# A decoder layer on one core: routing of the second tile's units moved between the first tile's, a 16-bit comparison, gate sums in rows, ring buffers given up one by one

## What is computed

```python
q = (hf @ w_q).reshape(T, 8, 2, 128)
sc = einsum('thpc,pkc->thpk', q, sub_keys)            # two lists of 128 key scores
v1, i1 = top_k(sc, 16)
cand = v1[:, :, 0, :, None] + v1[:, :, 1, None, :]    # pair sums
cidx = i1[:, :, 0, :, None] * 128 + i1[:, :, 1, None, :]
top, pos = top_k(cand, 16)
experts = take_along_axis(cidx, pos)                  # 128 experts for each token
gates = softmax(top)
a = gelu(einsum('cd,ced->ce', x, u[experts]))
y = einsum('ce,ced->cd', gates * a, v[experts])
```

## Time and profile before

| | |
|---|---|
| median of 3 runs | 947.8 us (945.09 to 950.91) |
| the profiled execution | 950.39 us |
| its span, first to last instruction | 948.6 us, 15685 instructions |
| mean granted TensorE clock | 0.945 |
| HBM read over the span | 343.80 MB, 364 GB/s |

### The profile page before, as it was taken

One profiled execution on the slowest core, in us unless ns is written; L12 is line 12 of the kernel. 1 busy time (PEld: TensorE's weight loads), 2 busy tenths in 40 slices (PEclk: granted clock), 3 DMA queues, 4 the chain that ended last, 5 costly groups with the idle time before them and its releaser, 6 DMA issues.

```text
span 948.6 us, 15685 instructions
## 1 busy us (share of the span) xinstructions
PE 849.3 (90%) x5808; PEld 548.5 (58%) x5808; DVE 648.5 (68%) x1485; ACT 417.2 (44%) x1049; POOL 386.9 (41%) x307
## 2 busy tenths in 40 slices
PE   8999999999988869887869999877897997998997
PEld 7999998799976524443446656342442551333333
DVE  5433686565557976887765787999989875444555
ACT  5534665544565653553433444444452332222252
POOL 1000065040004475565544435365664775343452
PEclk9999999999999999999989999787877997999999
DMA  8897533257336899999999999999899999999994
GB/s 307 229 202 210 183 125 134 89 223 266 134 111 224 350 414 404 404 415 407 342 383 414 414 412 406 373 374 366 310 397 390 376 415 415 417 414 401 402 346 187
DMA packets 55028, 303.20 MB, mean 320 GB/s; under 512 B 11515, under 2 KB 14959, under 8 KB 21777
## 3 DMA queue, kind: packets, MB, share of 16 engines
q0 software_dynamic: 37152, 225.29, 59.9%
q1 hardware_dynamic: 14968, 74.03, 21.8%
q10 hardware_dynamic: 2832, 2.88, 2.2%
HBM read 343.80 MB, written 1.54 MB: 364 GB/s over the span
## 4 chain that ended last, share of the span: by engine, by line
PE 38%; DMA 30%; DVE 15%; ACT 8%; issue 5%; POOL 3%; POOLq 0%; SPq 0%; DVEq 0%; ACTq 0%
DMA arena<-in_experts,arena 19%; PE y L1178 9%; DMA raw<-in_panels 6%; DVE late_ring L2179 5%; PE y L1249 4%; PE ps L792 4%; PE ps L794 3%; PE ps L793 3%; DVE w_lo L1748 3%; ACT w_hi L1331 2%; DMA late_ring<-in_experts,arena 2%; PE ps L835 2%; POOL arena L2387 2%; PE y L1137 1%; PE y L1302 1%
## 5 line engine op out<-in xcount | busy, mean ns | idle before, releaser
L2387 POOL DMA_INDIRECT arena<-in_experts,arena x167 | 223.5, 1338 | 168.1 <-PE ps L1181 124.9
L2179 DVE CUSTOM_DVE_ANT_0 late_ring<-arena 128x1024 f32<-128x1024 f32 x178 | 217.1, 1222 | 104.3 <-DMA arena<-in_experts,arena 100.4
L1181 PE MATMUL ps<-arena,diag 64*64 64x512 f32 x824 | 226.9, 678 | 0.0
L1178 PE MATMUL y<-arena,diag 64*64 64x512 f32 x528 | 146.2, 678 | 34.3 <-ACT diag L1565 34.2
L1178 PE MATMUL y<-late_ring,diag 64*64 64x512 f32 x424 | 118.3, 683 | 40.0 <-ACT diag L1565 39.9
L1551 ACT ACTIVATE acts<-dots 128x2 f32<-128x2 f32 x124 | 25.2, 203 | 290.5 <-DVE dots L2179 290.3
L1748 DVE TENSOR_TENSOR w_lo<-raw,w_hi 128x2048 fp32r<-128x2048 f32 x36 | 84.9, 2360 | 75.5 <-ACT w_hi L1331 75.5
L2179 DVE CUSTOM_DVE_ANT_0 late_ring<-late_ring,arena 128x1024 f32<-128x1024 f32 x73 | 89.3, 1223 | 37.2 <-DMA late_ring<-in_experts,arena 29.4
L2387 POOL DMA_INDIRECT late_ring<-in_experts,arena x55 | 71.5, 1299 | 99.9 <-PE ps L1181 89.0
L1178 PEld LDWEIGHTS y<-arena,diag 64*64 64x64 f32 x528 | 34.4, 144 | 114.3 <-ACT diag L1565 60.5
L1331 ACT CAST w_hi<-raw 128x2048 fp32r<-128x2048 f32 x37 | 70.5, 1905 | 62.7 <-DMA raw<-in_panels 49.4
(11 more groups left out here) (345 smaller groups left out, 1730.1 us busy)
## 6 DMA issues: line engine op xcount, KB each, us to landing
raw<-in_panels SPq DMA_DIRECT2D x40, 1024.0 KB, 5.1
arena<-in_panels SPq DMA_DIRECT2D x6, 1024.0 KB, 7.0
late_ring<-in_up SPq DMA_DIRECT2D x12, 512.0 KB, 8.3
late_ring<-in_experts SPq DMA_DIRECT2D x12, 512.0 KB, 7.8
x<-in_up SPq DMA_DIRECT2D x8, 512.0 KB, 8.6
x<-in_experts SPq DMA_DIRECT2D x8, 512.0 KB, 7.7
arena<-in_experts,arena POOLq DMA_INDIRECT x167, 14.4
arena<-line_scratch ACTq DMA_DIRECT2D x8, 320.0 KB, 9.0
```

What stands on the lines that cost most here:

```text
L1178: straight = pe.matmul(y[rows, t, cols], diag[rows, a % DIAGS, rows], slot(a)[rows, down], start=False, stop=False, skip_group_check=True)
L1181: across = pe.matmul(ps[to, half, :], diag[rows, b % DIAGS, rows], slot(b)[rows, down], start=first, stop=False, skip_group_check=True)
L2179: i = nc.vector.tensor_tensor_reduce(row if n < len(FIRST_BUFFERS) else products[s % GROUP], row, h_rows[:, u // PEER_HEADS, :], 1.0, 0.0, ...
L2387: nc.gpsimd.indirect_dma_start(out=slot(n), out_offset=None, in_=experts, in_offset=bass.IndirectOffsetOnAxis(ap=expert_rows(u)[:, s:s + 1 ...
```

## The change

It does these things:

- The order of routing becomes 0, 1, 2, 8, 3, 4, 9, 5, 10, 6, 7, 11, ... 15 (`ROUTED_AS`). Units 1 and 2 are early, over slots 0 to 8 and 9 to 18; all others are late, from slot 20 on, one per 8 slots (9 and 11 once each), and their steps are packed into 10 slots. Unit 15 begins at slot 120. Counts and waits go by the place in that order.
- Lists are turned and taken at slots 98 and 136; chunks begin at 110, 116, 122, 128 and then every 4 slots from 132 to 176; the down products are spread over groups 94 to 118.
- Buffers are given up one by one: 15 from slot 67, 14 from 71, 10 from 87, 11 from 97, 12 from 101. The ring has 13 or 14 buffers from slot 62 to 72, 12 or 13 to 101, and 10 from 105 on.
- There are 4 table places; the first two tables are loaded as soon as `x` is free, the next two when buffer 15 is.
- The places and 0 to 49 are compared as 16-bit values, with a 16-bit result (`is_pick`); a copy of `iota` is made once.
- Gate sums lie by block and token: PE writes its 20 columns 16 values apart, ACT copies, DVE weighs contiguous rows; the three products of `listed_gates` are one instruction.

The diff, cut:

```diff
-EARLY_ROUTED = 6
-LATE_ROUTES = {7: 78, 8: 86, 9: 94, 10: 102, 11: 110, 12: 118, 13: 127, 14: 136, 15: 145}
-LATE_STEPS = {1: 0, 2: 1, 3: 2, 4: 3, 6: 6, 7: 7, 8: 7, 9: 8, 10: 8, 12: 11, 13: 12, 14: 13}
+LATE_ROUTES = {8: 20, 3: 29, 4: 40, 9: 48, 5: 56, 10: 64, 6: 72, 7: 80, 11: 88, 12: 96, 13: 104, 14: 112, 15: 120}
+EARLY_ROUTES = {1: (0, 8), 2: (9, 18)}
+EARLY_ROUTED = len(EARLY_ROUTES)
+ROUTED_AS = {unit: n for n, unit in enumerate([0] + list(EARLY_ROUTES) + list(LATE_ROUTES))}
+LATE_STEPS = {1: 0, 2: 0, 3: 1, 4: 1, 6: 4, 7: 4, 8: 5, 9: 5, 10: 5, 12: 8, 13: 8, 14: 9}
...
-GATES_AT = {13: 1, 25: 2, 43: 3, 56: 4, 70: 5, 82: 6}
-SOFTMAX_BEHIND = {3: 2, 8: 3, 18: 4, 24: 5, 31: 6, 38: 7}
+GATES_AT = {10: 1, 19: 2}
+SOFTMAX_BEHIND = {3: 1, 8: 2}
...
-    RANKS_BEHIND[(begun + 3) // GROUP] = unit
-    TOP_BEHIND[(begun + 8) // GROUP] = unit
-    ROWS_BEHIND[(begun + 13) // GROUP] = unit
-    GATES_AT[begun + 14] = unit
+    RANKS_BEHIND[(begun + 1) // GROUP] = unit
+    TOP_BEHIND[(begun + 5) // GROUP] = unit
+    ROWS_BEHIND[(begun + 9) // GROUP] = unit
+    GATES_AT[begun + 10] = unit
...
-LISTS_BEHIND = {48: 0, 80: 1}
-LISTS_AT = {100: 0, 163: 1}
+LISTS_BEHIND = {47: 0, 66: 1}
+LISTS_AT = {98: 0, 136: 1}
...
-    begun = 114 + 6 * q if q < TOKEN_CHUNKS // 2 else 165 + 7 * (q - TOKEN_CHUNKS // 2) // 2
+    begun = 110 + 6 * q if q < 4 else 132 + 4 * (q - 4)
...
-    DOWN_BEHIND.setdefault(100 + b * 20 // BLOCKS, []).append(b)
+    DOWN_BEHIND.setdefault(94 + b * 26 // BLOCKS, []).append(b)
...
-GIVEN_BACK, GIVEN_FROM = (10, 11, 12, 14, 15), 62
+GIVEN_FROM = {15: 67, 14: 71, 10: 87, 11: 97, 12: 101}
...
-        if n == GIVEN_FROM:
-            waiting = [b for b in waiting if b not in GIVEN_BACK]
+        waiting = [b for b in waiting if GIVEN_FROM.get(b, SLOTS) > n]
         b = JOINS[n] if n in JOINS else waiting.pop(0)
-        if n < GIVEN_FROM or b not in GIVEN_BACK:
-            waiting.append(b)
+        waiting.append(b)
...
-        gate_sums = sb("gate_sums", [P, SUMS, 2, CHUNK * BLOCKS])
+        gate_sums = sb("gate_sums", [P, SUMS, BLOCKS, LISTED])
...
+        is_pick = work[:, TOPK * PAIRS // 2:].bitcast(BF16).rearrange("p (k c) -> p k c", k=TOPK)
...
-                   for at in (7 * D, 8 * D)]
-        tables = [x[:, 0, :], x[:, 1, :]] + [given[:, at:at + D] for at in (5 * D, 6 * D, 9 * D)]
+                   for at in (8 * D, 9 * D)]
+        tables = [x[:, 0, :], x[:, 1, :]] + [given[:, at:at + D] for at in (6 * D, 7 * D)]
...
-            sp.wait_ge(slot_free, LAST_GIVEN + 1)
             sp.wait_ge(ffn_sq_ready, 2 * TILES)
-            sp.wait_ge(taken["act"], taken_count(f"key_score{PEER_HEADS - 1}"))
-            sp.dma_start(count_row[:], count_in.to_broadcast([P, PEER_KEYS])).then_inc(count_in_place, 16)
             for j in range(2 * BLOCKS):
...
+                if j == TILES:
+                    sp.wait_ge(slot_free, LAST_IN[15] + 1)
+                if j == len(tables):
+                    sp.wait_ge(taken["act"], taken_count(f"key_score{PEER_HEADS - 1}"))
+                    sp.dma_start(count_row[:], count_in.to_broadcast([P, PEER_KEYS])).then_inc(count_in_place, 16)
...
+                sums = b[:, 0:CHUNK * BLOCKS].rearrange("p (b t) -> p b t", b=BLOCKS)
                 for j in range(CHUNK):
                     for piece in range(PIECES):
-                        mm = pe.matmul(b[:, j * BLOCKS:(j + 1) * BLOCKS], onehots[q % 2][:, :, j],
+                        mm = pe.matmul(sums[:, :, j], onehots[q % 2][:, :, j],
...
+                if j % 4 == 0:
+                    act.wait_ge(slot_free, LAST_IN[(14, 10, 12)[j // 4]] + 1)
...
-                late = u > EARLY_ROUTED
+                late = ROUTED_AS[u] > EARLY_ROUTED
...
-                    nc.vector.tensor_tensor(pick[:], top_atf[:].unsqueeze(2).to_broadcast([P, TOPK, PAIRS]),
-                                            iota[:].unsqueeze(1).to_broadcast([P, TOPK, PAIRS]), ALU.is_equal
+                    nc.vector.tensor_tensor(is_pick[:], top_places[:].unsqueeze(2).to_broadcast([P, TOPK, PAIRS]),
+                                            places[:].unsqueeze(1).to_broadcast([P, TOPK, PAIRS]), ALU.is_equal
...
+                elif q == 0:
+                    dve.wait_ge(slot_free, LAST_IN[11] + 1)
...
-                for piece in range(PIECES):
-                    nc.vector.tensor_tensor((gates_even, gates_odd)[k % 2][:, piece], in_block,
-                                            gate_piece[:, piece, tokens].unsqueeze(1).to_broadcast(shape), ALU.mult)
+                shape = [P, PIECES, BLOCKS, LISTED]
+                nc.vector.tensor_tensor((gates_even, gates_odd)[k % 2][:], in_block.unsqueeze(1).to_broadcast(shape),
+                                        gate_piece[:, :, tokens].unsqueeze(2).to_broadcast(shape), ALU.mult)
...
-                part_of_acts = in_block_acts[:, :, k * LISTED:(k + 1) * LISTED].rearrange(
-                    "p b (h t) -> p b h t", h=2)
-                sums = gate_sums[:, k % SUMS].rearrange("p h (t b) -> p b h t", b=BLOCKS)
-                nc.vector.tensor_tensor(part_of_acts, part_of_acts, sums, ALU.mult).then_inc(blocks_gated, 1)
+                part_of_acts = in_block_acts[:, :, k * LISTED:(k + 1) * LISTED]
+                nc.vector.tensor_tensor(part_of_acts, part_of_acts, gate_sums[:, k % SUMS], ALU.mult
```

73 lines of the change are left out of this document (42 added, 31 removed).

## The result

The median is 941.1 us (937.64 to 946.3, 20 runs) against 945.84 (942.39 to 952.16, 20 runs) for the kernel before: a ratio of 0.994, 95% interval 0.9923 to 0.9957. That is 5 us where 20 were forecast. It lies inside the range, near its upper end, and within the 1% that was called no change. The profiled execution has a span of 943.7 us, 4.9 less than before.

The account below looks back on a forecast made before the run. From about 330 to 930 us transfers bound the kernel at 415 GB/s, elsewhere DVE or PE. Terms 11 + 6 + 4.5 + 0.5 - 1 - 1 = 20 us took the median from 947.8 to 928 us; range 914 to 943.

Parts of the forecast that it names:

- What a stretch loses: Stretches below 415 GB/s: each loses its length times (415 - rate) / 415, put down to the engine that is full.
- The 11 us of the chunk stage: 598 to 700 us: DVE is the bound and 13.8 us are lost; with 2 to 3 left, 11 us gained.
- The 6 us of ring and tables: 450 to 490 us: more ring buffers and earlier tables replace 6.0 us of idle transfers; gain 6 us, 3 to 7.
- as balanced as before: no gain, no loss: Slots 74 to 114, up products: PE and transfers stay in balance, so neither gain nor loss there.
- The 4.5 us of the end: 890 to 930 us: PE bound by down products; spread over 26 groups, PE is no longer the bound, gain 4.5 us.
- The tail: From the last dot to its products: 4.1 us where some 2 are needed; 0.5 us counted, up to 2 possible.
- The start and tile 0's load: Start: units 1 and 2 press more steps between slots, 1 us lost; tile 0: DVE at 97%, 1 us lost, 0 to 6.
- rival A: Slots 20 to 74: DVE becomes the bound in tile 0, 8 us lost, 936 us, or 942; chance 0.12.
- Comparison and strided writes: DVE's 16-bit comparison stays at 0.99 us (0.57 by the one-hot's rate); PE's 48 strided gate products stay at 3.2 us.
- rival C: Chunks of gate products: strided PE writes overlap half as well, 6.8 us a chunk, 953 us, slower; chance 0.08.
- B: Chunk and down stages: the gain turns into other waits as faster DVE meets PE; 938 us, or 944; chance 0.14.
- D: 450 to 490 us: transfers were slow for another reason, the ring's part does nothing; 934 us, inside the forecast's 0.66.

Follow-up runs that it names:

- e8: Kernel after with calendar, giving-up of buffers and gate sums all as before; only early tables and 16-bit comparison stay: ratio 1.0015.
- e5: Kernel after with calendar and giving-up of buffers as before; cheaper gate sums, early tables and comparison stay: ratio 0.9945.
- e13: Kernel after with calendar and gate sums as before; ring, tables and comparison stay new: ratio 0.9991.
- e2: Kernel after with the calendar of before (routes, lists, chunks, down products at their old slots): ratio 0.9951.
- x6: Kernel after with one-hots of 8 keys in place of 128 from the third chunk on and one of three gate pieces multiplied: ratio 0.9911.
- e9: Kernel after with all tables waiting, as before, for the buffer and the last key score: ratio 0.9936.
- x4: Kernel after with half of the places compared, other picks becoming the first expert, so 13.3 MB more gathered: ratio 1.0233, 970.9 us.
- x3: Kernel after with only the first four up and four down tables loaded and reused, 18.9 MB left out: ratio 0.9705, 918.86 us.
- e7: Kernel after with up products two groups earlier, behind groups 35 to 54 in place of 37 to 56: ratio 0.992, 940.82 us.
- x1: Kernel after with one of three gate pieces multiplied, 16 gate products a chunk in place of 48: ratio 0.9932.
- e1: Kernel after with its five ring buffers given up at once at slot 62, as before: ratio 0.9945.
- e15: Kernel after with buffer 1 joining the ring at slot 192 in place of 79, nine buffers in place of ten: ratio 0.9959.

## Why the prediction was wrong

The direction was right, the size 4 times too large. The smaller mechanisms came as forecast; the terms of the three large gains did not. By its own steps:

**What a stretch loses.** This is the step that failed. I took the lost time as length x (415 - rate) / 415 and put all of it down to the one engine that was full, so that it would be had back when that engine was relieved. The three stretches gave 11 + 6 + 4.5 = 21.5 us in this way. In the chunk stage, relieving the full engine brought a part; ahead of the up products, what was won was held by the PE-bound stage behind it; over the down products, not PE but the bytes set the time. The idle share of the DMA engines, length x (1 - share) over the same rows, is 2.6 + 5.1 + 1.0 = 8.7 us, nearer to the outcome. But that is luck and no rule: from 450 to 470 us the rate rose by 21% (345 to 418) where the share rose by 6% (0.95 to 1.01).

**The 11 us of the chunk stage.** DVE was the bound there before, as I said, and the change took 21.6 us of DVE from this stage. It got 4.3 us shorter, and the time lost by my formula fell from 18.3 to 12.6 us, where I had expected 2 to 3 us to be left. The cheaper sums' 4.4 to 4.7 us of DVE gave 2.4 to 4.5 (`e8` and `e5`, `e13` and `e2`), the rest almost nothing, and 12 us less of DVE with 31 us less of PE gave 1.5 more (`x6`). The loss moved: DVE is full again in slots 120 to 136 (5.6 us lost), PE in slots 160 to 168 (2.8). My DVE sums were right in size: 9.1 + 7.3 + 1.5 + 1.6 = 19.5 us for 8 slots of units and chunks, and DVE was busy for 36.7 us in slots 120 to 136. What was wrong is the price that I put on it, 49 us of DVE against 47 of transfers and so 2 us.

**Gains that don't add.** Cheaper gate sums alone, and calendar with ring alone, bring the same 0.5% each, and together no more. I added terms that draw on one slack.

**The 6 us of ring and tables.** The transfers rose to 418 and 409 GB/s, and the wait of 5.2 us went, both as forecast; little of it was kept: slots 0 to 112 take 274.1 us, where they took 275.8. The four tables are 5.3 us of transfer, now ahead of slot 72, and the up products begin 178.1 us after slot 0's dot in place of 173.6. (The tables aren't all of this: `e9`, which loads them late, begins at 177.9.) From there PE sets the pace. The chain of waits of the kernel after, in the up stage:

```profile
506.29 3.65 PE ps L1231 x16
511.82 3.65 PE ps L1231 x16
517.35 3.65 PE ps L1231 x16
```

One product every 5.53 us, 20 in a row: 109.7 us from the first start to the last end, and 108.9 to 112.1 in every variant but `x4`, whatever has been loaded (`x3`: 110.0). The kernel before took 114.9, the first product's wait for its table among them. The last ends at 598.6, where it ended at 598.4. So the 7.1 us by which slots 72 to 112 became shorter are mostly the 5.4 by which they begin later. I had called the stage "as balanced as before: no gain, no loss" and yet let a gain pass through it. An earlier start of the gathers can't pass a stage that PE fills; an earlier start of the products could, though of the 6.6 us that `e7` won in this way only about 2 are seen in its time.

**The 4.5 us of the end.** PE is no longer the bound over the down products, as forecast (129.0 us of 147.4), but the stage is 3.2 us longer, not shorter. All sixteen kernels that load every table and gather no more have it between 145.8 and 147.9 us, with the old placing of the down products (`e2`, `e5`, `e8`, `e13`) and the new. Only fewer bytes shorten it (`x3`). It moves 58 to 60 MB, some 16 tables among them, at 396 to 410 GB/s. One more table lies in it than before, since 4 places and not 5 could be filled ahead (0.52 MB, 1.3 us); the rest of the 3.2 is not explained. My sum compared PE's 5.5 us a group with 4.2 us of transfers, which holds only for the groups behind the last table.

**The tail.** Forecast 0.5 and up to 2 us: it was 2.2. The words "up to 2 us more are there" were right, the value taken was low; `e2` and `e5`, with the old placing of the down products, have 9.0 and 9.1 us, `e8` has 9.6. So it doesn't come from that placing, as I had it. What it does come from was not tried.

**The start and tile 0's load.** Slot 0's dot is 1.0 us later, but single profiles have it anywhere from 304 to 311, so this isn't evidence. Tile 0's load of DVE cost nothing (`e9`: slots 0 to 72 in 157.7 us): rival A is out.

**Comparison and strided writes.** The comparison takes 990 ns against 0.99 us taken and 0.57 by the one-hot's rate: no gain. The rule of the Trainium skill ("Vector Engine (DVE) Microarchitecture Reference", section 5.1), one value a cycle where one input of such a 16-bit operation reads one element again and again, agrees with this. A chunk of gate products takes 3.18 us against 3.2: rival C is out.

**The rivals.** B, that the gain turns into other waits, is nearest with its 938 us, and its mechanism holds in part: PE takes DVE's place in slots 160 to 168, but with 20.7 us of PE less (`x1`) the stage is no shorter. D was right in its result (the ring's part does nothing: `e1`, `e13`); its reason, that the transfers at 450 to 490 us were slow for another cause, holds at least in part, as the old ring (`e1`) runs at 408 and 385 GB/s there, where the kernel before had 345 and 360.

**Two slips in the sums.** The lower end of the range, 914, isn't the sum given for it: 947.8 - 30.5 is 917. And the window showed 102 us / 43 = 2.37 us a slot, not the 2.45 that I took as confirmed.

**Open.** Why `x6`, with DVE and PE both at 70% in slots 136 to 160, still runs at 381 GB/s there and loses 4.5 us. A ring of ten in place of nine buffers makes no clear difference (`e15`), and four tables fewer don't shorten the stage (`x3`). Dips like that at 625 us, behind a wait of POOL for a buffer, would be the first thing to look at; a longer ring in these slots and another order of DVE's steps were not tried. Nor were the rows gathered there varied.

## What to carry to other kernels

Before a dip in GB/s is counted as a gain, cut the stretch into pieces of a few items of work and look in each for the engine that is full. In this kernel a stage at 384 GB/s on average was made of pieces at 343 to 417, with DVE full in one and PE in another; relieving the one that was full on average moved the loss elsewhere. The DMA share beside the rate is no measure of what can be had back. Cut both traces at the same item of work (here the dots of the slots), not at clock times; a stage bound by PE with a fixed amount of work swallowed what was won ahead of it. Where two edits feed on the same slack, test each alone and all of them undone but one: undoing one at a time showed no part that mattered.
